# Latent attention: values computed by tokens, query norm in the masking scale, rotary panels first, weights packed without gaps

## The reference

```python
cq, ckv, kr = jnp.split(h @ w_a, [384, 640], axis=-1)        # query latent, key/value latent, rotary key
cq, ckv = rms_norm(cq, g_q), rms_norm(ckv, g_kv)
q = (cq @ w_uq).reshape(B, L, 16, 64 + 32)                    # per head: 64 plain rows, 32 rotary rows
q_nope, q_rope = jnp.split(q, [64], axis=-1)
q_rope, k_rope = apply_rope(q_rope, cos, sin), apply_rope(kr[:, :, None, :], cos, sin)
kv = (ckv @ w_ukv).reshape(B, L, 16, 64 + 64)
k_nope, v = jnp.split(kv, [64], axis=-1)
# softmax(q.k / sqrt(96)) over earlier tokens, times v, 16 heads; then @ w_o
```

## Time and profile before

| | before |
|---|---|
| runs (us) | 1401.75, 1399.26, 1403.01; median 1401.75 |
| profiled execution | 1404.32 us, span 1402.4 us |
| mean granted clock of PE | 0.982 |
| PE busy | 1336.0 us, 95% of the span |
| DVE, ACT, POOL busy | 945.4, 811.3, 231.8 us |
| weights loaded | 378 units of 512 KB |
| share of PE in the chain that ended last | 84% |

### The profile page before, as it was taken

One profiled execution on the slowest core, in us unless ns is written; L12 is line 12 of the kernel. 1 busy time (PEld: TensorE's weight loads), 2 busy tenths in 40 slices (PEclk: granted clock), 3 DMA queues, 4 the chain that ended last, 5 costly groups with the idle time before them and its releaser, 6 DMA issues.

```text
span 1402.4 us, 30127 instructions
## 1 busy us (share of the span) xinstructions
PE 1336.0 (95%) x10433; PEld 1267.9 (90%) x10433; DVE 945.4 (67%) x1890; ACT 811.3 (58%) x1637; POOL 231.8 (17%) x216
## 2 busy tenths in 40 slices
PE   7899999999999999999986999999988999999997
PEld 6788999999977999999975899999987888999997
DVE  4665777765797777765685777776564566777754
ACT  5455676654666666654643567665463555766644
POOL 1000034420000044320010003442000000243400
PEclk9999999999999999999988999999998999999999
DMA  7332455556421456566330135655643333366662
GB/s 256 115 107 74 136 172 187 178 179 195 139 76 49 134 180 188 172 189 188 123 100 31 61 121 170 190 178 180 195 124 119 101 97 122 119 186 190 181 214 86
DMA packets 56867, 203.33 MB, mean 145 GB/s; under 512 B 6224, under 2 KB 8272, under 8 KB 56656
## 3 DMA queue, kind: packets, MB, share of 16 engines
q1 hardware_dynamic: 56784, 202.21, 46.1%
HBM read 201.13 MB, written 1.05 MB: 144 GB/s over the span
## 4 chain that ended last, share of the span: by engine, by line
PE 84%; DVE 7%; ACT 6%; issue 2%; DMA 1%; SPq 0%; DVEq 0%; ACTq 0%
PE ps L376 23%; PE ps L380 22%; PE ps L379 22%; PE ps L494 3%; PE ps L395 2%; PE ps L512 2%; PE ps L398 2%; PE ps L399 2%; DVE w_lo L1135 2%; PE ps L477 1%; PE ps L459 1%; ACT w_hi L765 1%; ACT probs L815 1%; DMA cst<-in_consts 1%; PE ps L577 1%
## 5 line engine op out<-in xcount | busy, mean ns | idle before, releaser
L1135 DVE TENSOR_TENSOR w_lo<-raw,w_hi 128x1024 fp32r<-128x1024 f32 x378 | 462.3, 1224 | 254.3 <-ACT w_hi L765 252.6
L376 PE MATMUL ps<-h_hi,w_hi 128*128 128x272 f32 (+1 forms) x1752 | 511.7, 292 | 7.7 <-DVE q_rope L1325 4.9
L765 ACT ACTIVATE w_hi<-raw 128x1024 fp32r<-128x1024 f32 x378 | 396.8, 1051 | 191.7 <-PE ps L376 180.0
L380 PE MATMUL ps<-h_hi,w_lo 128*128 128x272 f32 (+1 forms) x1752 | 504.8, 288 | 0.0
L379 PE MATMUL ps<-h_lo,w_hi 128*128 128x272 f32 (+1 forms) x1752 | 503.6, 287 | 0.0
L376 PEld LDWEIGHTS ps<-h_hi,w_hi 128*128 128x128 f32 x1752 | 330.8, 189 | 15.7 <-issue 5.9
L379 PEld LDWEIGHTS ps<-h_lo,w_hi 128*128 128x128 f32 x1752 | 331.4, 189 | 0.3
L380 PEld LDWEIGHTS ps<-h_hi,w_lo 128*128 128x128 f32 x1752 | 330.9, 189 | 0.0
L376 PE MATMUL ps<-hid_hi,w_hi 128*128 128x272 f32 (+2 forms) x676 | 198.1, 293 | 0.3 <-DVE y L1135 0.2
L379 PE MATMUL ps<-hid_lo,w_hi 128*128 128x272 f32 (+2 forms) x676 | 195.4, 289 | 0.0
L380 PE MATMUL ps<-hid_hi,w_lo 128*128 128x272 f32 (+2 forms) x676 | 195.4, 289 | 0.0
(11 more groups left out here) (153 smaller groups left out, 1751.2 us busy)
## 6 DMA issues: line engine op xcount, KB each, us to landing
raw<-in_weights SPq DMA_DIRECT2D x378, 512.0 KB, 3.7
cst<-in_consts SPq DMA_DIRECT2D x1, 1795.5 KB, 12.3
h<-in_x SPq DMA_DIRECT2D x2, 544.0 KB, 5.5
out<-h SPq DMA_DIRECT2D x8, 128.0 KB, 1.8
```

What stands on the lines that cost most here:

```text
L376: m = pe.matmul(b, whi, xhi, start=n == 0, stop=False)
L380: m = pe.matmul(b, wlo, xhi, start=False, stop=n == len(tiles) - 1)
L765: act.activation(w_hi[slot][:], raw[slot][:], ACT.Copy).then_inc(hi_ready, 1)
L1135: return dve.tensor_tensor(out_, a_, b_, op)
```

## The change

Four edits, all in layer 2. Values are computed by tokens: the latent is the stationary operand and 512 value columns move, so six panels (three chunks of tokens by two halves, the last chunk of 16 tokens) write `v_tok` rows directly; ACT scales them by the token's norm, and the value transposes and their copies go. For this the mean squares are needed by token too: `sum_squares` makes columns with one-column matmuls, and for the query norm only those. The query norm is no longer multiplied into q: it is the scale operand of the masking instruction (`q_scale`), so q leaves PSUM by plain copies on ACT (`take_q`). The four rotary panels stand first, two in a stage `r` before the values and two after them. In stage `qk` the tiles of a pair (3 and 2) follow each other without gaps, 46 tiles in 6 units; layer 2 has 23 units of `a`, `r`, `vt`, `qk` and `o` where it had 24. `mix` of pair m-3 now stands first in turn m of the loop, where `mix` of pair m-2 stood last.

```diff
-PAIR_TILES = (Q_LORA // P, KV_LORA // P, KV_LORA // P)
-ROPE_AFTER = 2
-RK = Q_LORA // P
+QT, KT = Q_LORA // P, KV_LORA // P
+ROPE_PANELS = 4
+def rope_head(name):
+    return Stage(name, [[(0, r * QT + k, k) for k in range(QT)] for r in range(2)], 1, banks=2)
 def latent_pairs(name):
-    one = [[(sum(PAIR_TILES[:w]) + k, k) for k in range(PAIR_TILES[w])] for w in range(3)]
-    rope = [[(r * RK + k, k) for k in range(RK)] for r in range(2)]
-    groups = [rope] + [one] * ROPE_AFTER + [rope] + [one] * (PAIRS - ROPE_AFTER)
-    return Stage(name, [[(u, t, k) for t, k in p] for u, g in enumerate(groups) for p in g], PAIRS + 2, banks=2)
-def pair_panel_at(m):
-    return 3 * m + (2 if m < ROPE_AFTER else 4)
-def rope_panel_at(r):
-    return r if r < 2 else 3 * ROPE_AFTER + r
+    sizes = [QT] * (ROPE_PANELS - 2) + [QT, KT] * PAIRS
+    first = [sum(sizes[:j]) for j in range(len(sizes))]
+    panels = [[((f + k) // DC, (f + k) % DC, k) for k in range(n)] for f, n in zip(first, sizes)]
+    return Stage(name, panels, -(-sum(sizes) // DC), banks=2)
...
-"mla": [whole("a", 6), latent_pairs("qkv"), whole("o", 8, 4)],
+"mla": [whole("a", 6), rope_head("r"), Stage("vt", [], 2, body=1), latent_pairs("qk"), whole("o", 8, 4)],
...
 def sum_squares(ks):
+    is_q = ks[0] == 0
     for k in ks:
         pe.wait_ge(lat_sq, k + 1)
-        pe.matmul(ps[:, 5 if k < 3 else 6, 0:T], ones, y[:, k % 4, :],
-                  start=k in (0, 3), stop=k in (2, 4)).then_inc(lat_sum, 1)
-def swap(src, done):
-    pe.wait_ge(bank_free, done)
+        if not is_q:
+            pe.matmul(ps[:, 6, 0:T], ones, y[:, k % 4, :], start=k == ks[0], stop=k == ks[-1])
+    cols = ((0, P), (N_META, N_META + P), (N_META + P, T)) if is_q else \
+        ((0, P), (P, 2 * P), (2 * P, T))
+    for n, (lo, hi) in enumerate(cols):
+        for k in ks:
+            ins = pe.matmul(ps[0:hi - lo, 5 if is_q else 4, n:n + 1], y[:, k % 4, lo:hi],
+                            ones[:, 0:1], start=k == ks[0], stop=k == ks[-1])
+    ins.then_inc(lat_sum, len(ks))
+def swap(src):
     pe.wait_ge(roped, n_swap[0])
     pe.matmul(ps[:, 7, 0:T], perm, src, start=True, stop=True).then_inc(swapped, 1)
     n_swap[0] += 1
 def after_a(i, j):
     if j == 3:
-        sum_squares(range(3))
+        sum_squares(range(QT))
     if j == 5:
-        sum_squares((3, 4))
-def latent_panel(j, first):
-    panel(sq, uq, pq, 0, j, from_latent(first), None, 0)
+        sum_squares(range(QT, QT + KT))
 def swap_rope(r):
-    if r >= 2:
-        pe.wait_ge(v_copied, n_v[0] + r - 1)
-    swap(y[:, 2 + r % 2, :], pq + rope_panel_at(r) + 1)
+    pe.wait_ge(bank_free, pr + r + 1)
+    swap(y[:, 2 + r % 2, :])
+def value_panel(n):
+    chunk, half = n // 2, n % 2
+    lo, hi = chunk * P, min(T, (chunk + 1) * P)
+    if n >= 2:
+        pe.wait_ge(vt_copied, n - 1)
+    out_ = ps[0:hi - lo, 2 + n % 2]
+    for k in range(KT):
+        slot = (uv + k) % RING
+        if n == 0:
+            pe.wait_ge(lo_ready, uv + k + 1)
+        whi, wlo = (w[slot][:, half * 512:half * 512 + 512] for w in (w_hi, w_lo))
+        xhi, xlo = (x[:, LAT + QT + k, lo:hi] for x in (hid_hi, hid_lo))
+        m = pe.matmul(out_, xhi, whi, start=k == 0, stop=False)
+        if n == 0 and k == 0:
+            m.then_inc(w_used, 1)
+        pe.matmul(out_, xlo, whi, start=False, stop=False)
+        m = pe.matmul(out_, xhi, wlo, start=False, stop=k == KT - 1)
+        if n == 5 and k == 0:
+            m.then_inc(w_used, 1)
+    m.then_inc(vt_done, 1)
 base = n_swap[0]
 gemm(a, "a", from_h, nr, after=after_a, lead=3)
-pe.wait_ge(bank_free, pa + 3)
-latent_panel(0, 0)
-swap(gated[:], pa + 6)
-latent_panel(1, 0)
-pe.wait_ge(bank_free, pa + 5)
+pe.wait_ge(bank_free, pa + 4)
+panel(sr, ur, pr, 0, 0, from_latent(0), None, 0)
+panel(sr, ur, pr, 0, 1, from_latent(0), None, 0)
+pe.wait_ge(bank_free, pa + 6)
+swap(gated[:])
+for n in range(6):
+    value_panel(n)
+    if n in (1, 3):
+        swap_rope(n // 2)
+for r in range(2):
+    panel(sq, uq, pq, 0, r, from_latent(0), None, 0)
 for m in range(PAIRS + 1):
-    p = pair_panel_at(m)
-    if m == 0:
-        latent_panel(p, 0)
-        swap_rope(0)
-    elif m < PAIRS:
-        latent_panel(p, 0)
+    p = pq + 2 + 2 * m
+    if m >= 3:
+        mix(a, kind, m - 3)
     if m == 1:
-        pe.wait_ge(roped, base + 2)
         pe.wait_ge(rope_key, 1)
+        pe.wait_ge(vt_copied, 6)
+        swap_rope(2)
     if m == 3:
-        pe.wait_ge(roped, base + 3)
-    if m == 5:
-        pe.wait_ge(roped, base + 4)
-    if m == 7:
-        pe.wait_ge(roped, base + 5)
+        swap_rope(3)
     if m:
-        pe.wait_ge(bank_free, pq + pair_panel_at(m - 1) + 2)
+        pe.wait_ge(roped, base + 2 + (m - 1) // 2)
+        pe.wait_ge(q_taken, m)
+        pe.wait_ge(bank_free, p)
         score(a, kind, 2 * m - 2)
         score(a, kind, 2 * m - 1)
+    if m < PAIRS:
+        panel(sq, uq, pq, 0, 2 + 2 * m, from_latent(0), None, 0)
     if m >= 2:
         turn(a, 2 * m - 4)
         turn(a, 2 * m - 3)
     if m < PAIRS:
-        latent_panel(p + 1, 3)
-        latent_panel(p + 2, 3)
-    if m == 0:
-        swap_rope(1)
-    if m == ROPE_AFTER - 1:
-        latent_panel(rope_panel_at(2), 0)
-        latent_panel(rope_panel_at(3), 0)
-    if m == ROPE_AFTER:
-        swap_rope(2)
-    if m == ROPE_AFTER + 1:
-        swap_rope(3)
-    if m:
-        pe.wait_ge(bank_free, pq + pair_panel_at(m - 1) + 3)
-        pe.wait_ge(roped, n_swap[0])
-        if m >= 2:
-            pe.wait_ge(v_copied, n_v[0] + m - 1)
-        turn_value(m - 1, 7)
+        panel(sq, uq, pq, 0, 3 + 2 * m, from_latent(QT), None, 0)
     if m == PAIRS:
         lead_o(a, kind, range(0, 5))
-    if m >= 2:
         mix(a, kind, m - 2)
-n_v[0] += 8
-pe.wait_ge(v_copied, n_v[0])
-lead_o(a, kind, range(5, O_LED))
+        lead_o(a, kind, range(5, O_LED))
...
+def take_r(r):
+    p = pr + r
+    act.wait_ge(panel_done, p + 1)
+    act.wait_ge(bank_free, p)
+    if r >= 2:
+        act.wait_ge(roped, ROPED0 + r - 1)
+    act.activation(y[:, 2 + r % 2, :], bank(p, 2), ACT.Copy).then_inc(bank_free, 1)
+def copy_vt(n):
+    chunk, half = n // 2, n % 2
+    rows = min(T, (chunk + 1) * P) - chunk * P
+    act.wait_ge(vt_done, n + 1)
+    if n == 0:
+        act.wait_ge(lat_scale, 1)
+    act.activation(v_tok[0:rows, chunk, half * 512:half * 512 + 512], ps[0:rows, 2 + n % 2],
+                   ACT.Copy, scale=lat_col[0:rows, 1, chunk:chunk + 1]).then_inc(vt_copied, 1)
+def take_q(m):
+    p = pq + 2 + 2 * m
+    act.wait_ge(panel_done, p + 1)
+    for s in range(2):
+        ins = act.activation(queries[0:HD, 2 * m + s, :], bank(p, 2)[HD * s:HD * s + HD], ACT.Copy)
+    ins.then_inc(q_taken, 1)
+for r in range(2):
+    take_r(r)
+split_unit(ur + AHEAD)
+for n in range(6):
+    copy_vt(n)
+    if n == 0:
+        split_unit(uv + AHEAD)
+split_unit(uv + 1 + AHEAD)
+for r in range(2):
+    split_panel(a, "qk", r)
+    take_r(2 + r)
 for m in range(PAIRS + 1):
     if m >= 3:
         out_hi(a, m - 3)
-    if m < PAIRS:
-        split_panel(a, "qkv", pair_panel_at(m))
     if m:
         exps(a, kind, 2 * m - 2)
-    if m >= 2:
+    if m < PAIRS:
+        take_q(m)
+        split_panel(a, "qk", 2 + 2 * m)
+    if m == PAIRS:
         copy_turned(a, 2 * m - 4)
         copy_turned(a, 2 * m - 3)
     if m:
         exps(a, kind, 2 * m - 1)
-    if m == ROPE_AFTER - 1:
-        split_panel(a, "qkv", rope_panel_at(2))
-    if m:
-        copy_value(m - 1, 7)
-n_v[0] += 8
+    if m < PAIRS:
+        split_panel(a, "qk", 3 + 2 * m)
+    if 2 <= m < PAIRS:
+        copy_turned(a, 2 * m - 4)
+        copy_turned(a, 2 * m - 3)
...
-in1=mask[0:r, cols], scale=-1.0,
+in1=mask[0:r, cols], scale=q_scale[0:r, ch:ch + 1] if kind == "mla" else -1.0,
...
+def scales():
+    dve.wait_ge(lat_std, 1)
+    dve.reciprocal(lat_col[0:N_META, 1, 2:3], lat_col[0:N_META, 1, 2:3])
+    dve.reciprocal(lat_col[:, 1, 0:2], lat_col[:, 1, 0:2]).then_inc(lat_scale, 1)
+    own.link(dve.reciprocal(q_scale[:], lat_col[:, 0, :]))
+    own.link(dve.tensor_scalar(q_scale[:], q_scale[:], -1.0, None, ALU.mult))
...
+def take_k(m):
+    p = pq + 3 + 2 * m
+    dve.wait_ge(panel_done, p + 1)
+    b = bank(p, 2)
+    tt(keys[0:64, 2 * m, :], b[0:64], kv_rstd[0:64], ALU.mult)
+    tt(keys[0:64, 2 * m + 1, :], b[64:128], kv_rstd[64:128], ALU.mult).then_inc(bank_free, 2)
+gemm(a, "a", close_latent, links=None, straight=True)
 n_swap += 1
 base = n_swap
-split_units(a, "qkv", 0, 0)
-take_r(0)
+assert base == ROPED0
+scales()
 rope_key_rows()
-latent_rstd(1)
-take_r(1)
-def take(m, which):
-    j = pair_panel_at(m) + which
-    dve.wait_ge(panel_done, pq + j + 1)
-    b = bank(pq + j, 2)
-    if which == 2:
-        if m >= 4:
-            dve.wait_ge(v_turned, n_v + m - 3)
-        tt(v_t(m), b, kv_rstd, ALU.mult).then_inc(bank_free, 1)
-        return
-    dst, by = ((queries, q_rstd), (keys, kv_rstd))[which]
-    tt(dst[0:64, 2 * m, :], b[0:64], by[0:64], ALU.mult)
```

(33 more changed lines are left out.)

74 lines of the change are left out of this document (42 added, 32 removed).

## The result

The changed kernel takes 1410.1 us (median of 8, 1406.7 to 1415.3) against 1402.8 (8 runs): ratio 1.0052, 95% interval 1.0030 to 1.0075. The forecast was 1399.8 with a range to 1407: the change makes the kernel slower, beyond the range. The profiled execution took 1413.2 us.

What follows compares the result with a forecast made beforehand. PE, busy 95% of the span, was taken to bound the kernel. 9.1 us won at full clock minus 6 us of clock gave 3 us, taken as 2 against the median 1401.75: 1399.8 us, range 1393 to 1407.

Steps and rivals of the forecast that it cites:

- Values by tokens: Layer 2 on PE: 36 matmuls of 512 columns add 8.1 us; eight turns lose 9.7 us of work.
- Mean squares by token: Before the loop on PE: 30 one-column instructions at 0.06 us cost 1.8 us (0 to 4.2), net +1.4.
- Rotary panels and the start: Ahead of the first scores: old waits go, waits of 1.0 and 2.9 us come; first scores at 725.0, 5.6 later.
- Scale operand: Masking instructions: reading the scale from a column costs 0 to 0.1 us for each of 48; taken as 0.
- ACT's round, `rope_r`: Loop: ACT paces turns at 7.4 or 8.4 us; `rope_r` makes PE wait 3.3 at turn 3's swap, 4.2 at `mix`.
- The clock takes most of it back: Layer 2: new idle brings three clock falls, 20 us at half, costing 6 us of the 9.1 won.
- the count of falls: Layer 2: three falls of 6.8 us each, counted because falls seen had followed waits of 2.2 to 5.7 us.
- The sign given for being wrong, half clock in the ordinary turns: Loop: half clock in ordinary turns was listed among the observations that would show the forecast wrong.
- The 9.1 us won at `lead_o`: End of the loop: `lead_o` at 789.0 instead of 798.1, summed at the full clock.
- the forecast's 789.0: Start of `lead_o` at the full clock: first scores at 725.0, then a loop of 64.0 us.
- rival 3: Loop: clock falls in ordinary turns, each further stretch costs 2 to 3 us; three or four give 1407; chance 0.22.

Runs made afterwards that it cites:

- pool_late: Changed kernel with GpSimd's four rotary-key copies held until VectorE has roped the first query panel; 1407.9 us, ratio 1.0038.
- after_filled: Changed kernel with matmuls without use placed on PE ahead of each of its waits in layer 2; 1400.8 us, ratio 0.9985.
- before_filled: Kernel before with matmuls without use ahead of two rotary swaps and of `turn_value` in turns 2 and 3; 1397.5 us, ratio 0.9965.
- best_norm: all_best with VectorE's `take_k` and `normalise` ahead of the weight-unit split in every turn; 1383.5 us, ratio 0.9877.
- start_best: Changed kernel with query one-column sums one panel later, GpSimd's key copies behind `rope_r(0)`, VectorE's first keys ahead of the weight split; 1407.0 us, ratio 1.0032.
- qsum_late: Changed kernel with the one-column sums of the query latents behind panel 4 of stage `a` instead of panel 3; 1408.6 us, ratio 1.0043.
- all_best: start_best plus `mix` behind the scores, key panel ahead of the probability transposes, fourth swap behind turn 3's key panel; 1392.2 us, ratio 0.9925.

## Why the prediction was wrong, by its own steps

- *Values by tokens*: right. The 36 matmuls take 8.35 us at their distance of 0.232, forecast 8.1.
- *Mean squares by token*: this term was mis-sized. The 30 instructions take 4.4 us instead of 1.8 in the profiled execution; at the full clock 1.93 + 1.06 = 3.0. With the longer wait and the panel matmuls behind them partly at the lower clock too, this part of the start lost 6.0 us to the old one, where 1.4 were counted. Of the excess about 1.2 us are the price of the instructions and about 3 the clock.
- *Rotary panels and the start*: the waits foreseen came in place and size (0.70 for 1.0; 2.79 for 2.9). One was missed: POOL's copies in the way of `rope_r(0)`, 1.74 us at the second swap. So the first scores begin at 731.2, not at 725.0.
- *Scale operand*: 0.06 us each, inside its bounds; taken as 0 in the sum, and the time agrees.
- *ACT's round, `rope_r`*: right. The swap waits 3.26 us for 3.3, `mix` of pair 3 4.55 for 4.2; an ordinary turn takes 7.81 for 7.4 (pool_late), and the loop at the full clock (after_filled) 64.6 for 64.0.
- *The clock takes most of it back*: this step failed. Forecast were three falls, 20 us at half and 6 us of time on top of the loop's 64.0. Measured were five, 41.0 us at half, 34.1 of them in the loop, which takes 78.7 us: 14.1 us more than in after_filled, 0.41 for each us at half. Two stretches were 10.2 us long where 6.8 were taken, and two waits of 1.6 and 2.0 us that the count of falls left out were followed by one each. The sign given for being wrong, half clock in the ordinary turns, is what came (760.46, behind 1.64 us). The step also priced one us at 0.3, where all executions give 0.38, and on average the changed kernel has 8.3 us more of the lower clock than the old one, where the sum had 7.3 less. The 9.1 us won at `lead_o` compare a new path at the full clock with an old one of which 21.5 us (7.84 + 6.82 + 6.83) ran at half. At one clock the forecast's 789.0 stands against 792.3 (before_filled), so about 3 us were to be won by the path itself, and the late start turned them into a loss.

In the two profiles `lead_o` comes 11.8 us later, where the forecast had it 3 us earlier: 6.2 us of that miss are the start (4.6 the squares, 1.7 the missed wait) and 8.7 the loop, nearly all of it clock. So 1410 is what rival 3 described (the clock falls in ordinary turns, 1407), with a longer start on top.

## What to carry to other kernels

Compare a forecast and a trace at the same clock, and judge the clock over many executions, not by one profile. Moving one wait on the busiest engine mostly names another; what paid was an order in which each hand-over (keys, turned probabilities) has an engine's other work in front of it, and on the helper engines whatever the busiest one waits for ahead of what it does not (best_norm: 1383.5 us, 1.2% under the kernel before, with every part of the change kept). That does not show that the change pays: no run gave the old kernel the same new orders, and none took the four edits apart beyond the one-column products and the scale operand.

## What the runs showed of the hardware

- A VectorE product of 128x272 with both inputs in SBUF took 1.33 instead of 0.43 us while GpSimd copied, and four additions of 32x272 took 3.80 instead of 1.77; with one input in PSUM a product took 0.43.
- A one-column fp32 matmul instruction (two make a product) with a 128x128 stationary operand costs 0.09 us at 2.4 GHz twelve in a row (1.06 us) and 0.11 eighteen in a row (1.93), 0.19 at mostly 1.2 GHz (3.34 for eighteen). 64 columns wide it costs 0.11 at 2.4 GHz (1.26 us for twelve).
- Executions of one kernel differ by up to 13 us (start_best 1396.3 to 1409.5), and three quarters of the variance go with the time at the lower clock.
- Waits of PE behind which or in which the clock fell were 0.5 to 5.7 us long, but a wait of 1.64 us was followed by a fall in one execution (760.8) and by none in another (pool_late, 759.3). In qsum_late (700.9) and all_best (701.2) it fell with no wait over 0.21 us in the 5 us ahead.
